# A weight unit of expert 28 loaded in sixteen transfers of eight partitions

## The chip, the cores and the metric

The kernel runs on one core of a Trainium2 chip. The metric is the device time of one execution in microseconds (us), the median of several executions.

## The reference

One decoder layer over 256 tokens of width 1024, in float32. A mixer (eight attention heads with forget gates beside a causal depthwise convolution) is added to the input; then comes a mixture of 32 experts, of which each token uses four:

```python
hn = rmsnorm(h, norm_ffn_g)
for e in range(32):                       # gates: softmax over the top 4 logits, else 0
    g, u = split(hn @ w_gu[e] + b_gu[e])  # w_gu[e]: 1024 x 2048
    act = (clip(u) + 1.0) * (min(g, 7) * sigmoid(1.702 * g))
    out += gates[:, e] * (act @ w_down[e] + b_down[e])   # w_down[e]: 1024 x 1024
return rmsnorm(h + out, norm_final_g)
```

An expert has 12 MB of weights, all 32 have 384 MB, and each is read once.

## The kernel before, in words

The mixer and the routing take the first 130 us or so. Then TensorE goes through the experts in order. For each it gathers up to 64 of its tokens, multiplies them with the expert's weights, and adds the results to the residual in PSUM. TensorE's stream is written out by hand in the functions `up`, `down`, `bias`, `gather_rows`, `scatter` and so on (L1484 to L1742); nearly all of its matmuls are recorded at one line, L1223, the helper `mm`.

The weights come in **units** of 1 MB: 128 partitions by 8 KB. An expert has eight units for its first matrix (`up`) and four for its second (`down`). `SEQUENCE` lists the units in order of use; the last two experts are interleaved: up of 30, up of 31, down of 30, down of 31. The units go into `ring`, 22 places of one unit each in SBUF. TensorE counts the units that it has finished with in the semaphore `units_used`; the sync engine (SP) waits for a place to be free and then issues the next load (loop at L466 and on, issue at L445).

A **load** is one DMA of one or more neighbouring units (`load_sizes`, L121): four units for most experts (packets of 32 KB to a partition), two from expert 28 on (`FINE_FROM` = 336, the first unit of expert 28; packets of 16 KB), one for the last ten units. A load that wraps around the end of the ring is cut in two (`pieces`). Twenty semaphores `load_full` serve the loads in turn; `landed(k)` is the count at which load k is all there, 16 for each DMA. TensorE waits for it in `arrived_unit` (L1564) before the first unit of the load. So a unit that landed can be used only once its whole load has landed.

All of these DMAs are issued on one queue, SP's. A DMA over 128 partitions is dealt to all sixteen DMA engines, eight partitions each, and each engine goes through its share of the queue by itself: none waits for another. A load has landed when the last engine is through with its share. The program's own instructions are fetched over the same engines (queues q8 and q14 of the profile).

After the last expert, both token blocks are normalised with `final_gain` (a last DMA on SP, L490) and written out (L504, L507).

Of the kernel before, what the change touches and what calls it, by code (L numbers as in the profile page):

```python
# [34 lines left out]
P = 128  # L35
# [16 lines left out]
def hybrid_layer(nc, x, norm_mix_g, w_in, b_f, b_glu, w_dw, b_dw, ln_g, ln_b, w_out, norm_ffn_g,  # L52
# [27 lines left out]
    UP_UNITS, DOWN_UNITS = KB, FB // 2  # L80
    UNITS = UP_UNITS + DOWN_UNITS
# [12 lines left out]
    SPARES = (UP_SPARE, DOWN_SPARE, ROW_SPARE)  # L94
# [3 lines left out]
    SINGLES, FINE_UP_TO, FINE_FROM = (UNITS * 2 + 8, UNITS * 3 + 2), UNITS * 8, UNITS * (E - 4)  # L98
# [14 lines left out]
    def unit_at(n):  # L113

        return FIRST_LAP.index(n) if n < LAP_END else (n - LAP_END) % RING

    def used_for(n):

        return FIRST_LAP[n - LAP_END] + 1 if n < LAP_END + RING else n - RING + 1
# [16 lines left out]
    LOADS = [(sum(SIZES[:k]), size) for k, size in enumerate(SIZES)]  # L136
    FIRSTS = {first: k for k, (first, _) in enumerate(LOADS)}
    LOAD_SEMS = 20

    def pieces(k):  # L140

        first, size = LOADS[k]
        size_here = min(size, RING - unit_at(first))
        return [(first, size_here)] + ([(first + size_here, size - size_here)] if size_here < size else [])

    def landed(k):

        return 16 * sum(len(pieces(j)) for j in range(k % LOAD_SEMS, k + 1, LOAD_SEMS) if LOADS[j][0] not in SPARES)

    assert all(sum(LOADS[k - LOAD_SEMS]) <= used_for(sum(LOADS[k]) - 1) for k in range(LOAD_SEMS, len(LOADS)))  # L150


# [2 lines left out]
    with ExitStack() as ctx:  # L155
# [3 lines left out]
        def sem(name):  # L159
            return ctx.enter_context(nc.semaphore(name))  # L160
# [127 lines left out]
        piece_in = {name: sem(f"{name}_in") for name in PIECES[2:]}  # L288
        load_full = [sem(f"load_full{s}") for s in range(LOAD_SEMS)]
        units_used, spare_in = sem("units_used"), sem("spare_in")  # L290
# [91 lines left out]
        def _(sp):  # L382
# [14 lines left out]
            for name in PIECES[2:]:  # L397
                if name.startswith("out"):
                    first = D_ATT if name == "out_conv" else 0
# [21 lines left out]
            def rows_of(first, size):  # L421

                e, u = SEQUENCE[first]
                return weight_rows(e, u, size)

            def weight_rows(e, u, size):
                if u < UP_UNITS:
                    g, b = u // 4, u % 4
                    return w_gu[e, 4 * P * g:4 * P * (g + 1), :].rearrange("(p b) n -> p b n", b=4)[:, b:b + size, :]
                f = 2 * (u - UP_UNITS)  # L430
                return w_down[e, :, :].rearrange("(p b) n -> p b n", b=FB)[:, f:f + 2 * size, :]

            def ring_rows(first, size, rows):
                return ring[:, unit_at(first) * UNIT:(unit_at(first) + size) * UNIT].rearrange("p (b n) -> p b n", b=rows)

            def load(k):

                for first, size in pieces(k):
                    from_ = rows_of(first, size)
                    if first == LAST_UNIT:  # L440
                        halves_ = ring_rows(first, size, from_.shape[1])
                        sp.dma_start(halves_[:, 0, :], from_[:, 0, :]).then_inc(load_full[k % LOAD_SEMS], 16)
                        sp.dma_start(halves_[:, 1, :], from_[:, 1, :]).then_inc(last_row_in, 16)
                        continue
                    sp.dma_start(ring_rows(first, size, from_.shape[1]), from_).then_inc(load_full[k % LOAD_SEMS], 16)  # L445

# [19 lines left out]
            for k, (first, size) in enumerate(LOADS):  # L466
                if first >= UNITS * E:
                    break
                if first in SPARES:
                    continue  # L470
                if first >= LAP_END:
                    sp.wait_ge(units_used, used_for(first + size - 1))
                elif first in released:
                    for used in released[first]:
                        sp.wait_ge(*used)
                load(k)
                if first == FIRST_LAP[2 * CONV_SLOT]:
                    sp.wait_ge(bgu_ready, 2)
                    load_spare_row(0)
                if first == FIRST_LAP[2 * KEYS_SLOT]:  # L480
                    load_up_spare()
                if first == FIRST_LAP[2 * PIECE_SLOT["out_conv"] + 1]:
                    load_down_spare_rest()
                if first == LAP_END - 1:
                    sp.wait_ge(route_done, 2)
                    load_spare_row(1)
                    load_down_spare()
# [4 lines left out]
            def extra(e, r, o):  # L492

                sp.wait_ge(units_used, o * UNITS + UNITS * E)
                for k, (first, size) in enumerate(LOADS):
                    if first >= UNITS * E:
                        from_ = weight_rows(e, first - UNITS * E, size)
                        sp.dma_start(ring_rows(first, size, from_.shape[1]), from_).then_inc(load_full[k % LOAD_SEMS], 16)

# [721 lines left out]
        def _(pe):  # L1221
# [342 lines left out]
            def arrived_unit(n, o=None):  # L1564

                if n in SPARES:
                    pe.wait_ge({UP_SPARE: up_spare_in, DOWN_SPARE: down_spare_in, ROW_SPARE: spare_in}[n], 32)
                elif n in FIRSTS:
                    k = FIRSTS[n]
                    pe.wait_ge(load_full[k % LOAD_SEMS], landed(k) if o is None else o * 16 + landed(k))  # L1570
# [213 lines left out]
```

## Time and profile before

| | us |
|---|---|
| median of 3 runs (lowest to highest) | 1038.83 (1038.70 to 1039.03) |
| profiled execution, its own time | 1038.4 |
| its span, first to last instruction | 1036.7 |
| TensorE busy | 1006.8 (97%) |
| share of the sixteen DMA engines in use | 96.7% by SP's queue |
| granted TensorE clock, mean | 0.994 of full speed |

The span is 1.7 us shorter than the time of its own execution, and that execution is 0.4 us under the median. Sums below are made against the span and carried over to the median. TensorE is busy nearly all the time, and so are the DMA engines. Which of the two holds the other up changes along the way, and that can be read only stretch by stretch.

### The profile page before, as it was taken

How to read it: one execution, taken by the hardware profiler on the slowest of the kernel's cores; microseconds unless marked ns; L12 is line 12 of the kernel's file. 1: busy time of each engine (PE TensorE's matmuls, PEld its weight loads, DVE VectorE, ACT ScalarE, POOL GpSimd, SP SyncE). 2: the span in 40 equal slices, each digit the busy share in tenths (PEclk: the TensorE clock that was granted, in tenths of full speed). 3: DMA queues.
4: the chain of work that ended last, by engine and by line, in shares of the span. 5: the costliest groups of instructions: out<-in, count | busy, mean ns of one | idle time of the engine just before them, and what ended most of it. 6: DMA issues, size and time to landing. Idle time of an engine off the chain costs nothing.

```text
span 1036.7 us, 11001 instructions
## 1 busy us (share of the span) xinstructions
PE 1006.8 (97%) x4821; PEld 398.2 (38%) x4822; DVE 242.2 (23%) x532; ACT 163.3 (16%) x303; POOL 15.0 (1%) x28
## 2 busy tenths in 40 slices
PE   9999999999999999999999999899999999899997
PEld 7875534333333333333333333333333333233332
DVE  3995341211011111111111212111111112011112
ACT  6144321111011111111110111010111101011102
POOL 4000000000000000000000000000000000000000
PEclk9999999999999999999999999999999999999999
DMA  9995789999999999999999999999999999999995
GB/s 309 391 421 198 277 342 399 417 415 428 427 426 434 426 434 428 435 425 434 426 435 426 435 427 431 432 429 428 433 429 429 433 428 431 425 428 426 425 422 223
DMA packets 34987, 421.62 MB, mean 407 GB/s; under 512 B 4237, under 2 KB 8633, under 8 KB 14714
## 3 DMA queue, kind: packets, MB, share of 16 engines
q1 hardware_dynamic: 33370, 420.57, 96.7%
q8 instruction: 39, 0.64, 0.2%
q10 hardware_dynamic: 1568, 0.33, 0.2%
q14 instruction: 10, 0.08, 0.0%
HBM read 419.82 MB, written 1.05 MB: 406 GB/s over the span
## 4 chain that ended last, share of the span: by engine, by line
PE 71%; DMA 21%; DVE 7%; ACT 1%; issue 0%; DVEq 0%; ACTq 0%
PE work L1223 60%; DMA ring<-in_w_gu 21%; PE resid L1223 7%; DVE main L917 4%; PE work L1531 1%; PE work L1605 1%; PE work L1561 0%; DMA main<-in_x 0%; PE work L1342 0%; PE work L1252 0%; PE work L1441 0%; DVE main L924 0%; DVE ring L896 0%; DVE ring L927 0%; DVE main L971 0%
## 5 line engine op out<-in xcount | busy, mean ns | idle before, releaser
L1223 PE MATMUL work<-ring,main 128*64 128x512 f32 (+1 forms) x3080 | 687.0, 596 | 17.4 <-DMA ring<-in_w_gu 15.9
L1223 PEld LDWEIGHTS work<-ring,main 128*64 128x64 f32 (+1 forms) x3080 | 219.1, 138 | 460.7 <-issue 411.3
L1126 DVE TENSOR_SCALAR main<-work 128x512 f32<-128x512 f32 x32 | 22.1, 692 | 554.5 <-PE work L1223 554.5
L757 ACT ACTIVATE main<-main 128x512 f32<-128x512 f32 x32 | 20.2, 632 | 434.6 <-DVE main L1126 434.6
L1223 PE MATMUL work<-ring 128*128 128x256 f32 (+2 forms) x308 | 71.8, 403 | 0.9 <-DVE ring L927 0.8
L1223 PE MATMUL resid<-main 128*128 128x512 f32 (+1 forms) x136 | 68.0, 618 | 0.8 <-ACT main L820 0.8
L1223 PE MATMUL work<-bgu_rows,ident 128*64 128x512 f32 (+1 forms) x260 | 61.0, 587 | 0.8 <-DVE main L1126 0.8
L1223 PEld LDWEIGHTS work<-ring 128*128 128x128 f32 (+1 forms) x308 | 55.6, 186 | 15.7 <-issue 8.7
L775 ACT ACTIVATE main<-work 64x512 f32<-64x512 f32 x60 | 35.5, 592 | 126.9 <-PE work L1223 126.2
L1119 DVE TENSOR_SCALAR lent<-count,place,gates 128x64 f32<-128x64 f32 x68 | 17.9, 310 | 155.3 <-PE work L1561 147.5
L917 DVE SCALAR_TENSOR_TENSOR main<-ring,main 128x256 f32<-128x256 f32 x116 | 46.6, 480 | 1.3 <-ACT main L631 1.1
L1223 PE MATMUL work<-main,select 128*64 128x512 bf16 x360 | 44.0, 379 | 0.0
L1133 DVE SCALAR_TENSOR_TENSOR main<-main 128x512 f32<-128x512 f32 x32 | 34.1, 1066 | 1.1
L1223 PEld LDWEIGHTS work<-main,select 128*64 128x64 bf16 x360 | 21.1, 110 | 29.7 <-issue 17.9
L762 ACT ACTIVATE main<-work 128x512 f32<-128x512 f32 x32 | 19.1, 597 | 72.3 <-PE work L1605 72.3
L1223 PEld LDWEIGHTS resid<-main 128*128 128x128 f32 (+1 forms) x136 | 19.6, 189 | 27.8 <-issue 27.8
L1223 PE MATMUL resid<-ring,main 128*128 128x512 f32 (+1 forms) x68 | 28.8, 571 | 0.0
L772 ACT ACTIVATE main<-work 128x256 f32<-128x256 f32 x17 | 6.5, 384 | 140.1 <-PE work L1561 140.1
L1223 PEld LDWEIGHTS work<-bgu_rows,ident 128*64 128x64 f32 x260 | 18.3, 137 | 24.4 <-issue 9.0
L1139 DVE TENSOR_TENSOR main<-work,cols 128x512 f32<-128x512 f32 x30 | 20.7, 691 | 13.1 <-PE work L1531 13.1
L1130 DVE TENSOR_TENSOR main<-main 128x512 f32<-128x512 f32 x32 | 22.2, 692 | 5.8 <-ACT main L757 5.8
L1531 PEld LDWEIGHTS work<-ident,lent 128*128 128x128 f32 x120 | 12.6, 140 | 24.3 <-issue 24.3
(200 smaller groups left out, 332.3 us busy)
## 6 DMA issues: line engine op xcount, KB each, us to landing
ring<-in_w_gu SPq DMA_DIRECT2D x33, 4096.0 KB, 39.3
ring<-in_w_gu SPq DMA_DIRECT2D x40, 2048.0 KB, 18.2
ring<-in_w_down SPq DMA_DIRECT2D x16, 4096.0 KB, 39.5
ring<-in_w_down SPq DMA_DIRECT2D x13, 2048.0 KB, 15.1
ring<-in_w_down SPq DMA_DIRECT2D x23, 1024.0 KB, 27.8
ring<-in_w_gu SPq DMA_DIRECT2D x22, 1024.0 KB, 18.9
ring<-in_w_gu SPq DMA_DIRECT2D x7, 3072.0 KB, 35.5
ring<-in_w_down SPq DMA_DIRECT2D x4, 3072.0 KB, 38.1
```

Of the source, the lines that this page charges most:

```text
L757: nc.scalar.activation(sig_h, gate_h, ACT.Sigmoid, scale=SWIGLU_ALPHA).then_inc(sig_ready, 1)
L762: nc.scalar.activation(to, work[:, act_bank(n), :], ACT.Copy).then_inc(act_t_ready, 1)
L775: return nc.scalar.activation(y_sb[buffer][h][parity * CAP:(parity + 1) * CAP, :], work[h * CAP:(h + 1) * CAP, bank, :], ACT.Copy)
L917: V.scalar_tensor_tensor(acc, u_pad[:, c, j:j + SEQ], dw_cols[:, c, j:j + 1], acc, ALU.mult, ALU.add)\
L1119: done = V.tensor_scalar(weighted[:, t, parity * CAP:(parity + 1) * CAP], count[:, bass.ds(r * CAP, CAP)], place[:, t, bass.ds(e, 1)], gat ...
L1126: V.tensor_scalar(gate_h, work[:, GATE_BANK, :], SWIGLU_LIMIT, None, ALU.min).then_inc(gate_clamped, 1)
L1130: V.tensor_tensor(sig_h, sig_h, gate_h, ALU.mult).then_inc(glu_ready, 1)
L1133: V.scalar_tensor_tensor(gate_h.rearrange("p (b j) -> p j b", b=4), up_h.rearrange("p (j b) -> p j b", b=4), 1.0, sig_h.rearrange("p (j b) ...
L1139: V.tensor_tensor(tok_t.rearrange("p (h b) c -> p b h c", b=4), work[:, OUT_BANK, :].rearrange("p (b h c) -> p b h c", b=4, h=2), cols[:, ...
L1223: return nc.tensor.matmul(out_, lhsT, rhs, start=start, stop=stop, skip_group_check=True)
L1531: last = nc.tensor.transpose(work[:, OUT_BANK, b * P:(b + 1) * P], tok_rows[:, b // 2, b % 2 * P:(b % 2 + 1) * P], ident[:, :])
L1605: last = nc.tensor.transpose(work[:, act_bank(n), j * P:(j + 1) * P], gate_h[:, j * P:(j + 1) * P], ident[:, :])
```

## The change

Load 336 (units 0 and 1 of expert 28, 2 MB) was one DMA of 128 partitions with 16 KB each. Now its first unit is one DMA of 128 partitions with 8 KB each, and its second unit is sixteen DMAs, each of eight partitions with 8 KB each. All seventeen count on the load's semaphore; `landed` counts them. Bytes, places and order stay as they were. A DMA over eight partitions is dealt to eight engines, one partition each.

```diff
+    BY_EIGHTS = (FIRSTS[FINE_FROM],)
+    EIGHT = 8
...
+    def transfers(k):
+
+        return len(pieces(k)) + (P // EIGHT if k in BY_EIGHTS else 0)
+
     def landed(k):
 
-        return 16 * sum(len(pieces(j)) for j in range(k % LOAD_SEMS, k + 1, LOAD_SEMS) if LOADS[j][0] not in SPARES)
+        return 16 * sum(transfers(j) for j in range(k % LOAD_SEMS, k + 1, LOAD_SEMS) if LOADS[j][0] not in SPARES)
...
                 for first, size in pieces(k):
                     from_ = rows_of(first, size)
+                    if k in BY_EIGHTS:
+                        to = ring_rows(first, size, size)
+                        sp.dma_start(to[:, 0:size - 1, :], from_[:, 0:size - 1, :]).then_inc(load_full[k % LOAD_SEMS], 16)
+                        for p in range(0, P, EIGHT):
+                            sp.dma_start(to[p:p + EIGHT, size - 1, :], from_[p:p + EIGHT, size - 1, :]).then_inc(load_full[k % LOAD_SEMS], 16)
+                        continue
```

## Rows read from the trace of the kernel before

**Rows 1.** The page: busy time of TensorE, DMA packets, and queues (packets, MB, share).
```profile
PE 1006.8 (97%) x4821; PEld 398.2 (38%) x4822; DVE 242.2 (23%) x532; ACT 163.3 (16%) x303; POOL 15.0 (1%) x28
...
q1 hardware_dynamic: 33370, 420.57, 96.7%
q8 instruction: 39, 0.64, 0.2%
```

**Rows 2.** The chain that ended last, 840 to 905 us: start, us, what.
```profile
849.29 3.61 PE work L1223 x16
852.90 0.02 issue
852.92 43.88 DMA ring<-in_w_gu
896.79 0.04 issue
896.84 8.35 PE work L1223 x29
```

**Rows 3.** The same chain, shares by line, 905 us to the end.
```profile
by line: PE work L1223 79.1%; PE resid L1223 9.4%; PE work L1531 1.8%; PE work L1605 1.8%; PE work L1561 1.0%; DVE main L1205 1.0%; ACT work L577 0.9%; DVE main L1212 0.6%; ACT main L831 0.5%; DVE main L1126 0.5%; ACT main L820 0.5%; issue 
```

**Rows 4.** Waits of the whole span, then of 905 us to the end: total us, times, longest.
```profile
PEld work L1223 <- DMA ring<-in_w_gu: 25.1, 12, 3.4
PE work L1223 <- DMA ring<-in_w_gu: 15.9, 11, 2.6
...
PEld work L1223 <- DMA ring<-in_w_gu: 0.8, 2, 0.5
```

**Rows 5.** Stretches: us, busy of PE, PEld, DVE, ACT, POOL, clock, DMA share, GB/s.
```profile
895.00:920.00 25.00, 23.16 (x104) 8.02 (x106) 4.59 (x9) 2.65 (x5) 0.00 (x0) 0.93 1.01 429
920.00:945.00 25.00, 25.00 (x122) 8.79 (x120) 4.52 (x10) 2.57 (x5) 0.00 (x0) 1.00 1.00 425
945.00:970.00 25.00, 25.00 (x122) 8.84 (x120) 3.74 (x5) 3.02 (x5) 0.00 (x0) 1.00 1.01 427
```

**Rows 6.** Issue L445 at 864.9 us (load 336), then at 941.5 us: issue ns, us to landing.
```profile
L445 SPq DMA_DIRECT2D ring<-in_w_gu x1: 328/328/328, 864.9 to 864.9; - x1
...
DMA to landing us min/median/max: 46.5/46.5/46.5
...
L445 SPq DMA_DIRECT2D ring<-in_w_gu x1: 2452/2452/2452, 941.5 to 941.5; - x1
...
DMA to landing us min/median/max: 43.9/43.9/43.9
```

**Rows 7.** TensorE in order of time: start, us, line, operation, tiles, count [idle before].
```profile
919.04 13.95 PE L1223 MATMUL work<-ring,main 128*64 128x512 f32 x64
...
982.17 7.09 PE L1223 MATMUL work<-ring,main 128*64 128x512 f32 x32
...
985.41 0.38 PEld L1223 LDWEIGHTS work<-ring,main 128*64 128x64 f32 x4 [0.47 <-DMA ring<-in_w_gu]
```

**Rows 8.** DMA share (tenths) and GB/s in 40 slices of 1016 to 1027 us.
```profile
DMA  9998999998777775566445454554444220000000
GB/s 372 417 447 358 432 462 432 372 402 328 328 313 313 313 298 238 238 253 238 179 179 194 179 209 179 209 209 194 179 179 164 119 104 30 30 0 0 0 0 0
```

**Rows 9.** Queues in 538 to 542 us, then in 59.3 to 60.0 us.
```profile
q8 instruction: 1, 0.02, 1.7%
...
q10 hardware_dynamic: 8, 0.01, 3.4%
```

**Rows 10.** SP: short DMAs of L391 (issue ns), order of time at 866 to 900 us, waits at 860 to 1010 us.
```profile
L391 SPq DMA_DIRECT2D ring<-in_w_dw x2: 316/366/417, 3.4 to 3.8; - x2
...
870.51 12.24 SPq L445 DMA_DIRECT2D ring<-in_w_gu  x3
887.07 4.14 SPq L445 DMA_DIRECT2D ring<-in_w_down  x2
894.31 0.33 SPq L445 DMA_DIRECT2D ring<-in_w_gu  x1
...
SPq L445 <- PE work L1223: 105.6, 26, 8.2
```

**Rows 11.** Issues by size: count, KB each, median us to landing.
```profile
result<-main SPq DMA_DIRECT2D x2, 256.0 KB, 2.0
ring<-in_w_gu SPq DMA_DIRECT2D x22, 1024.0 KB, 18.9
```

More of the change, by code:

```diff
@@ L144, in pieces @@
         return [(first, size_here)] + ([(first + size_here, size - size_here)] if size_here < size else [])
+    def transfers(k):
+        return len(pieces(k)) + (P // EIGHT if k in BY_EIGHTS else 0)
     def landed(k):
-        return 16 * sum(len(pieces(j)) for j in range(k % LOAD_SEMS, k + 1, LOAD_SEMS) if LOADS[j][0] not in SPARES)
+        return 16 * sum(transfers(j) for j in range(k % LOAD_SEMS, k + 1, LOAD_SEMS) if LOADS[j][0] not in SPARES)
+    assert all(len(pieces(k)) == 1 and LOADS[k][1] > 1 and LOADS[k][0] % UNITS < UP_UNITS for k in BY_EIGHTS)
     assert all(sum(LOADS[k - LOAD_SEMS]) <= used_for(sum(LOADS[k]) - 1) for k in range(LOAD_SEMS, len(LOADS)))
```

## The prediction, made before the result was known

> **What bounds the kernel now.** I read the page first. TensorE is busy 97% of the span and SP's DMA queue fills 96.7% of the sixteen engines [rows 1]; as averages these say only that both are nearly full. So I went to the chain that ended last. Until 896.8 us it comes back once in two experts to a weight load: its last such piece runs from 852.92 for 43.88 us and ends in TensorE's start at 896.84 [rows 2]. That stretch is bound by the DMA engines. From 905 us to the end the chain has no DMA in it at all: 79.1% is TensorE at the experts' matmuls, and the rest is TensorE's other work and the closing normalisation [rows 3]. The waits say the same. TensorE waited 15.9 us for loads in the whole span, 11 times; after 905 us it waited for none, and only two weight loads (which run ahead of the matmuls) waited, 0.8 us together [rows 4]. In the stretches 920 to 945 and 945 to 970 us TensorE is busy 25.00 of 25 us, at full clock, while the DMA engines are full too, at 425 to 427 GB/s [rows 5].
>
> The reason for the switch at 897 us is the size of the loads. The loads are smaller from expert 28 on, so a unit no longer waits for three neighbours. The DMA engines are no faster than before.
>
> The changed load is number 336. It was issued at 864.9 us and landed 46.5 us later, at 911.4 [rows 6]; TensorE first uses it at 919.04 [rows 7]. Everything that the change touches thus lies behind the last DMA wait of TensorE, in the part that TensorE bounds. What matters is how much room is left there. The tightest place I find is the fourth load of expert 30, issued at 941.5 and landed 43.9 us later, at 985.4 [rows 6]. Its first matmul is the 17th of the 32 that begin at 982.17 and take 7.09 us: 982.17 + 16 x 7.09 / 32 = 985.7. The weight load before it did wait 0.47 us, until 985.41, and no matmul was held up [rows 7]. So the room is 0.3 us there. At every other load behind the changed one it is more.
>
> **When a load lands.** It lands with its last engine, and the engines don't run together. At the end of the stream the share of busy engines falls from full to a half between 1018.7 and 1021.2 us, stays near a half until 1024.5, and reaches nothing at 1025.1 [rows 8] (slices of 0.275 us). So there is an early group of about eight engines and a late group of eight, some 4 us behind. A cause is in the trace: 39 instruction fetches of 16 KB on queue q8 [rows 1]. One of them takes 1.7% of 16 engines x 4 us = 1.1 us of one engine [rows 9]. Some 33 fetches fall after 150 us, when the stream hardly pauses any more; if only eight engines serve them, each loses 33 / 8 x 1.1 = 4.5 us. That is about the gap.
>
> **Which group gets the extra bytes** decides the sign. The kernel has two other transfers that are dealt to eight engines (8 KB each, issued on ScalarE's queue, q10). The first shows as 8 packets in 59.3 to 60.0 us [rows 9]. No view names a packet's engine. But on a busy engine the next packet starts where the last one ended, so the packet records can be strung into sixteen chains. I did that around this transfer: the engine that served the third q8 fetch is none of those that carry its packets, and neither are the two engines that were furthest behind at that time, as the first two fetches would leave them. I take it that the eight-row transfers use the group without fetches, the early one. The records before and after an idle queue can't be strung together, so this is a likely reading and no certain one.
>
> The Trainium skill ("DMA: Bandwidth & Descriptors", on why a DMA increments its semaphore by 16) says that such a transfer from SP uses the lowest-numbered engines, as many as divide its rows. The eight packets agree with the count of eight; which numbers they are, no row shows, and the page doesn't say which engines fetch instructions.
>
> **The change part by part.**
>
> *Bytes.* The second unit puts 128 KB on each of eight engines instead of 64 KB on each of sixteen. At 425 GB/s for sixteen engines [rows 5] one moves 26.6 KB/us (thousand bytes), so 65,536 bytes are 2.5 us. The early group gets 2.5 us later, the late group 2.5 us earlier. From load 336 on the late group (gap about 4 us) is then ahead of or level with the early one, and loads land 1.5 to 2 us sooner. Value in the span: 0, since no matmul waits there. What it adds is room at the 985 us place, 0.3 us before and about 2 us after.
>
> *Sixteen completions instead of one.* Below, nothing: completions of the neighbouring loads already pass between packets, and the share stays at 1.00 or more with 1 MB and 2 MB loads mixed [rows 5]. Above, each of the sixteen could hold its engines for the whole 2.0 us that a store on an idle queue takes from issue to landing [rows 11]; sixteen of them would be 32 us. I take nothing, as loads queued behind each other are the nearest row, and keep up to 0.1 us each (1.6 us) for the range.
>
> *SP's issue time.* Seventeen issues instead of one. The nearest short DMAs took SP 316 and 417 ns [rows 10], so 16 x 0.37 = 5.9 us more; SP is free of the load at about 871.2 instead of 865.3 us. Next in its queue is load 338, issued at 870.51 before: 0.7 us late. In 860 to 1010 us SP waited 105.6 us for TensorE to free places [rows 10], so it catches up at the next wait. Its lead over the landing is 46.5 us [rows 6]. Cost 0. If the cover of that lead were gone, it would be the 5.9 us.
>
> *Room in the queue.* Later issues of SP take up to 2.45 us [rows 6] where others take 0.33, so the queue has a limit. The early engines get 16 x 2 more entries (a packet and a completion each) in place of 8. SP will be held up sooner, in 870 to 905 us, and stand some loads further back. With more than 40 us queued before it I expect that half of that remains. Cost 0; the bound above is in the rivals.
>
> *TensorE's wait* is for one higher count, the same instruction. Cost 0.
>
> Sum: 0 on a span of 1036.7, thus 1038.4 for the profiled execution, 1038.8 for the median. In other executions the room of 0.3 us may be used up (they took up to 0.4 us longer), and the change could then give back up to 0.4 us. I stay with 1038.8.
>
> **The rivals.**
>
> *Slower: the late group gets the bytes.* If the low eight are the late ones, or some of them are, every load from 336 on lands 2.5 us later. It decides where the room is under 2.5 us, above all at 985.4: the matmul due at 985.7 starts at 987.9, and 2.5 - 0.3 = 2.2 us go straight through to the end; later loads then have the 2.2 us more. 1038.8 + 2.2 = 1041.0. For it: my chains are strung by nearness in time. Against it: three fetches of three, all on engines outside the eight. 10%.
>
> *Slower: small transfers or a full queue.* Each of the sixteen holds its engines for some time of its own, or SP, held up by the queue's limit, lets the engines run dry. At the bound of 2.0 us each it is 32 - 0.3 = 31.7 us, 1070.5; it shows from 0.15 us each on (16 x 0.15 = 2.4). Against it: the landings of 22 loads of 1 MB, 18.9 us after issue in the median [rows 11], with full engines, which shows many in flight at once. 5%. The Trainium skill (same page, the rules for kernel authors) says that transfers under 64 KB pay mostly overhead and that its measured 64 KB transfer took 0.95 us; each of the sixteen is just 64 KB. By that, run one after the other, they would take 15.2 us. The trace speaks against its use here, since it is a figure for one transfer alone.
>
> *Faster: earlier landings count.* If the median execution, unlike the profiled one, waits in the last 140 us, the 1.5 to 2 us come off: 1037.0. Against it: the three runs lie within 0.33 us, and the profiled one is 0.4 us under them. 4%; more than 0.2% only if other loads gain too, 2%.
>
> *It doesn't do what it says.* The eight-row DMAs are spread over sixteen engines, and nothing moves: 1038.8. The eight packets of q10 are against it. 4%.
>
> **How the numbers follow.** My forecast has 77%, the other cases 10, 5, 4 and 4. 0.2% is 2.1 us, about what a measurement of this kernel can tell from no change. Within it lie the forecast, the last two rivals but for 2%, and a part of the first (2.2 us is just over it; 2% of its 10). Faster 0.02, same 0.85, slower 0.13. The forecast's own range is 1038.2 to 1039.3. With the bound of 1.6 us for the completions, the earlier landings, and the first rival it is 1037.4 to 1041.1.
>
> **What would show it.** In the profile after: the last DMA wait of TensorE still at 896.8; no wait of 905 us or later; load 336 landing at about 909.5; the load issued near 941.5 landing near 983.7 and no 0.47 us before its weight load; in the last stretch the groups' two falls in share closer together, the last at about 1023.5. A DMA wait of about 2 us near 986 us, with landings 2.5 us later, would prove my reading of the groups wrong. SP issues of some us each between 871 and 905 are expected and should cost nothing.

## The result and the profile after

Over four executions the changed kernel took 1047.01 us in the median (1045.92 to 1047.87), the kernel before 1038.93 us (1038.70 to 1039.47) in the same job. The ratio is 1.0073 with a 95% interval of 1.0056 to 1.0089: 8.1 us slower, where no change was forecast. The profiled execution took 1047.87 us with a span of 1046.0, 9.3 us more than the span of before. The lines of code have moved: L445 is now L458, L1223 is L1236, the changed load is issued on L449 (its first unit) and L451 (the sixteen transfers).

The page, its busy times and queues, against [rows 1]:
```profile
PE 1007.4 (96%) x4821; PEld 397.2 (38%) x4822; DVE 242.3 (23%) x532; ACT 163.0 (16%) x303; POOL 14.9 (1%) x28
...
q1 hardware_dynamic: 33626, 420.57, 96.6%
```
TensorE does the same work in 0.6 us more (1006.8 us before). SP's queue moves the same bytes in 256 more packets and is as full as before. So all but 0.6 of the 9.3 us is idle time of TensorE, and yet no engine of the DMA has become idle. The page alone shows no cause.

The chain that ended last, 840 us to the end (start, us, what), against [rows 2] and [rows 3]:
```profile
854.92 41.85 DMA ring<-in_w_gu
...
918.75 1.08 SPq L458
919.83 0.04 issue
919.88 45.17 DMA ring<-in_w_gu
...
998.17 4.12 SPq L458
1002.29 0.36 issue
1002.65 30.29 DMA ring<-in_w_down
```
Up to 896.8 us it is the chain of before: the load on it was issued 2.0 us later (854.92 against 852.92), but TensorE starts within 0.02 us of the same time (896.82 against 896.84). Then it has DMA in it twice more, where it had none after 905.

TensorE's matmuls after 905 us that waited for a load (start, us, line, operation, tiles, count [idle before and its releaser]):
```profile
921.31 3.65 PE L1236 MATMUL work<-ring,main 128*64 128x512 f32 x16 [2.21 <-DMA ring<-in_w_gu]
925.85 3.65 PE L1236 MATMUL work<-ring,main 128*64 128x512 f32 x16 [0.89 <-DMA ring<-in_w_gu]
930.74 3.65 PE L1236 MATMUL work<-ring,main 128*64 128x512 f32 x16 [1.24 <-DMA ring<-in_w_gu]
935.64 3.65 PE L1236 MATMUL work<-ring,main 128*64 128x512 f32 x16 [1.25 <-DMA ring<-in_w_gu]
960.12 3.65 PE L1236 MATMUL work<-ring,main 128*64 128x512 f32 x16 [0.83 <-DMA ring<-in_w_gu]
965.09 3.65 PE L1236 MATMUL work<-ring,main 128*64 128x512 f32 x16 [1.32 <-DMA ring<-in_w_gu]
1032.98 3.65 PE L1236 MATMUL work<-ring,main 128*64 128x512 f32 x16 [0.30 <-DMA ring<-in_w_down]
```
Seven waits, 8.0 us; before there was none [rows 4]. The first is for the changed load itself, which lands at 921.3 instead of 911.4 us. The next load lands at 925.8 (issued 883.2, 42.6 us to landing); before it was 916.3 (870.5 + 45.8). It is 9.5 us late too. From there on the loads come only as fast as the engines move them, and TensorE meets the delay in pieces.

Where the delay arises, the table of stretches shows (columns as in [rows 5]; the last two are the DMA engines' share and GB/s). The first line is of the kernel before, the others are of the kernel after:
```profile
900.00:920.00 20.00, 20.00 (x98) 7.00 (x96) 4.59 (x9) 2.65 (x5) 0.00 (x0) 0.98 1.00 425
...
860.00:900.00 40.00, 37.17 (x168) 12.35 (x168) 5.32 (x13) 4.50 (x8) 0.00 (x0) 0.96 1.00 427
900.00:920.00 20.00, 19.09 (x92) 6.61 (x88) 4.60 (x9) 2.67 (x5) 0.00 (x0) 0.99 1.01 272
920.00:945.00 25.00, 20.32 (x98) 7.19 (x100) 4.51 (x9) 2.54 (x5) 0.00 (x0) 1.00 1.00 425
945.00:970.00 25.00, 22.85 (x110) 7.47 (x108) 1.21 (x2) 1.67 (x3) 0.00 (x0) 1.00 1.01 425
```
Between 900 and 920 us the engines are as busy as ever (share 1.01) and move 272 GB/s, not 425. This is the stretch in which the sixteen transfers are served. The packet records say how: a packet of 8 KB takes 314 ns in the median from 895 to 900 us and 656 ns from 908 to 912; in those four microseconds one of 16 KB takes 613 ns in the kernel before and 1288 ns here. Those of 16 KB belong to whole loads. Of the 323 packets of 8 KB or more that began between 904 and 920 us, every one took over 15% longer than packets of its size take at the full rate (313, 614 and 915 ns for 8, 16 and 24 KB); of those that began from 896 to 903 us none did. So packets on all sixteen engines slow down, not only those of the changed load.

The working for the whole: (425 - 272) x 20 / 425 = 7.2 us lost by the rate, minus the room of 0.3 us, is 6.9 of the 9.3 us measured in the span. That leaves 2.4 us. The 2.5 us for the bytes on engines that carry more, if a late one is among them, would fill them, but that this is their source is not shown (see "Which group gets the bytes" below). The question for the experiments was what halves the rate.

SP's queue in order of time (start, us, line, operation, count), against [rows 10]:
```profile
866.95 0.33 SPq L449 DMA_DIRECT2D ring<-in_w_gu  x1
867.32 15.86 SPq L451 DMA_DIRECT2D ring<-in_w_gu  x16
883.23 11.78 SPq L458 DMA_DIRECT2D ring<-in_w_gu  x3
```
The sixteen issues take 15.9 us, the last two 2.4 us each. SP is held up, as expected. But the first slow packet begins at 903.0 us, some 20 us after the last of these issues, and no engine runs dry, so this is not the cause.

### The profile page after: what moved, and what is told of

Same layout as the page of the kernel before. It is cut to its first block, busy times and chain, and to the rows that moved or that the text cites. A ratio compares the mean times of both kernels' runs of the same rounds, so it can differ in the third digit from the quotient of the medians.

```text
span 1046.0 us, 11017 instructions
## 1 busy us (share of the span) xinstructions
PE 1007.4 (96%) x4821; PEld 397.2 (38%) x4822; DVE 242.3 (23%) x532; ACT 163.0 (16%) x303; POOL 14.9 (1%) x28
## 3 DMA queue, kind: packets, MB, share of 16 engines
HBM read 419.82 MB, written 1.05 MB: 402 GB/s over the span
## 4 chain that ended last, share of the span: by engine, by line
PE 69%; DMA 28%; DVE 1%; SPq 0%; ACT 0%; issue 0%; DVEq 0%; ACTq 0%
PE work L1236 59%; DMA ring<-in_w_gu 25%; PE resid L1236 7%; DMA ring<-in_w_down 3%; PE work L1544 1%; PE work L1618 1%; SPq L458 0%; DMA main<-in_x 0%; PE work L1574 0%; PE work L1355 0%; PE work L1265 0%; PE work L1454 0%; DVE main L984 0%; DVE main L964 0%; DVE main L1218 0%
## 5 line engine op out<-in xcount | busy, mean ns | idle before, releaser
L1236 PE MATMUL work<-ring,main 128*64 128x512 f32 (+1 forms) x3080 | 686.6, 595 | 26.1 <-DMA ring<-in_w_gu 24.3
L1236 PEld LDWEIGHTS work<-ring,main 128*64 128x64 f32 (+1 forms) x3080 | 217.9, 138 | 471.0 <-issue 408.8
L1236 PE MATMUL work<-ring 128*128 128x256 f32 (+2 forms) x308 | 71.8, 403 | 0.9 <-issue 0.8
L1236 PE MATMUL resid<-main 128*128 128x512 f32 (+1 forms) x136 | 68.9, 624 | 0.8 <-ACT main L833 0.8
L1236 PE MATMUL work<-bgu_rows,ident 128*64 128x512 f32 (+1 forms) x260 | 61.0, 587 | 0.8 <-DVE main L1139 0.8
L1236 PEld LDWEIGHTS work<-ring 128*128 128x128 f32 (+1 forms) x308 | 55.6, 186 | 15.7 <-issue 8.7
L1236 PE MATMUL work<-main,select 128*64 128x512 bf16 x360 | 44.0, 379 | 0.0
L1236 PEld LDWEIGHTS work<-main,select 128*64 128x64 bf16 x360 | 21.2, 110 | 29.7 <-issue 17.9
L1236 PEld LDWEIGHTS resid<-main 128*128 128x128 f32 (+1 forms) x136 | 19.9, 191 | 27.8 <-issue 27.8
L1236 PE MATMUL resid<-ring,main 128*128 128x512 f32 (+1 forms) x68 | 28.8, 571 | 0.0
L1236 PEld LDWEIGHTS work<-bgu_rows,ident 128*64 128x64 f32 x260 | 18.3, 137 | 24.4 <-issue 9.0
```

What stands on the lines that cost most here:

```text
L1236: return nc.tensor.matmul(out_, lhsT, rhs, start=start, stop=stop, skip_group_check=True)
```

## The experiments

All of them change only how load 336 is brought in (2 MB, two units of 128 partitions). Three groups of four were run, with the kernel before at 1038.84, 1038.83 and 1038.88 us. In all twelve profiles the DMA engines stay full from 900 to 945 us (share 0.94 to 1.05 in every stretch read). The tables below have the columns of [rows 5].

**First group: is it the layout on one side, or the number of transfers?** In the kernel after, each small transfer writes eight neighbouring partitions from eight neighbouring rows. First, both sides four apart, so that eight transfers stay in partitions 0 to 63 and eight in 64 to 127:
```diff
-                            sp.dma_start(to[p:p + EIGHT, size - 1, :], from_[p:p + EIGHT, size - 1, :]).then_inc(load_full[k % LOAD_SEMS], 16)
+                            base = 32 * (p // 32) + p % 32 // EIGHT
+                            sp.dma_start(to[base:base + 29:4, size - 1, :], from_[base:base + 29:4, size - 1, :]).then_inc(load_full[k % LOAD_SEMS], 16)
```


> The sixteen transfers take eight partitions each that are four apart (base, base + 4, ... base + 28) on both sides, instead of eight neighbours; same bytes, same count, same eight engines per transfer. Theory A (eight engines write into neighbouring partitions of SBUF at once and get into each other's way there): the slow packets go, time within 1 us of before, 1038.5 to 1039.5. Theory B (eight engines read neighbouring rows of 8 KB in HBM at once): the same, so this run alone doesn't part A from B. Theory C (each small transfer costs its engines time, wherever it writes): as the changed kernel, about 1047. Theory D (the late engines got the extra bytes): 1041 to 1047, with landings 2.5 us later than before.

Measured: 1046.16 us (1045.47 to 1047.61), ratio 1.0076 [1.0059, 1.0093]. In the time it is the kernel after. In the table of stretches it is not:
```profile
900.00:903.00 3.00, 3.00 (x18) 0.95 (x14) 0.00 (x0) 0.00 (x0) 0.00 (x0) 1.00 1.05 442
904.00:911.00 7.00, 7.00 (x38) 2.69 (x34) 2.81 (x4) 1.63 (x3) 0.00 (x0) 1.00 1.05 234
914.00:918.00 4.00, 2.52 (x12) 0.63 (x8) 0.86 (x4) 1.41 (x3) 0.00 (x0) 1.00 0.99 233
```
The first transfers, to partitions 0 to 63, run at the full rate (8 KB packets at 312 ns, 88 of them from 900 to 904 us). From about 904 us, with the first transfer to partitions 64 to 127, it is 234 GB/s. From 914 to 918 us only the engines that lag furthest are still at the small transfers (10 packets of 8 KB begin in it), and the rate is as low as before.

Then only one side four apart:
```diff
+                            sp.dma_start(to[base:base + 29:4, size - 1, :], from_[p:p + EIGHT, size - 1, :]).then_inc(load_full[k % LOAD_SEMS], 16)
```


> Only the side in SBUF takes partitions four apart; the side in HBM reads eight neighbouring rows as in the changed kernel (so the rows of this unit stand in other partitions than they should; bytes and times are the same). Theory A (writes into neighbouring partitions): fast, 1038.5 to 1039.5. Theory B (reads of neighbouring rows): slow, about 1047. Theory C (small transfers as such): slow, about 1047.

```diff
+                            sp.dma_start(to[p:p + EIGHT, size - 1, :], from_[base:base + 29:4, size - 1, :]).then_inc(load_full[k % LOAD_SEMS], 16)
```


> Only the side in HBM reads rows four apart; the side in SBUF writes eight neighbouring partitions as in the changed kernel (so the rows of this unit stand in other partitions than they should). Theory A (writes into neighbouring partitions): slow, about 1047. Theory B (reads of neighbouring rows): fast, 1038.5 to 1039.5. Theory C: slow, about 1047.

And the load in two DMAs of 128 partitions:
```diff
-                        for p in range(0, P, EIGHT):
-                            sp.dma_start(to[p:p + EIGHT, size - 1, :], from_[p:p + EIGHT, size - 1, :]).then_inc(load_full[k % LOAD_SEMS], 16)
+                        sp.dma_start(to[:, size - 1, :], from_[:, size - 1, :]).then_inc(load_full[k % LOAD_SEMS], 16)
```


> The load is cut in two as in the change, but its second unit is one DMA over 128 partitions: no transfer of eight partitions is left. All theories expect the time of before, 1038.5 to 1039.5; another time would put the cause on the cut itself (8 KB instead of 16 KB packets, one more completion).

Measured: 1045.95 us, ratio 1.0070 [1.0054, 1.0087], with the SBUF side alone four apart; 1046.29, 1.0077 [1.0060, 1.0094], with the HBM side alone; and 1039.42, 1.0006 [0.9996, 1.0016], with two whole DMAs, which keep 422 GB/s from 900 to 920 us. The first shows the two halves of the run above (399 GB/s at 900 to 903, 258 at 904 to 911); the second is slow throughout (289 GB/s at 900 to 920). The stretch in the second and in the run with two whole DMAs:
```profile
900.00:920.00 20.00, 18.17 (x89) 6.65 (x87) 4.61 (x9) 3.39 (x6) 0.00 (x0) 1.00 1.01 289
...
900.00:920.00 20.00, 20.00 (x98) 7.08 (x96) 4.59 (x9) 3.39 (x6) 0.00 (x0) 1.00 1.00 422
```
What follows: the HBM side changes nothing, neither kind of neighbour alone is the cause, and splitting the load costs nothing if each part spans 128 partitions. Which partitions are written matters, and so far in step with the half of SBUF.

**Second group: which partitions, and does it need small transfers?** One half of the partitions comes in one DMA of 64 rows, the other in sixteen transfers of eight rows:
```diff
-                        sp.dma_start(to[:, 0:size - 1, :], from_[:, 0:size - 1, :]).then_inc(load_full[k % LOAD_SEMS], 16)
-                        for p in range(0, P, EIGHT):
-                            sp.dma_start(to[p:p + EIGHT, size - 1, :], from_[p:p + EIGHT, size - 1, :]).then_inc(load_full[k % LOAD_SEMS], 16)
+                        sp.dma_start(to[64:P, :, :], from_[64:P, :, :]).then_inc(load_full[k % LOAD_SEMS], 16)
+                        for n in range(P // EIGHT):
+                            base = 0 + 32 * (n % 8 // 4) + n % 4
+                            sp.dma_start(to[base:base + 29:4, n // 8, :], from_[base:base + 29:4, n // 8, :]).then_inc(load_full[k % LOAD_SEMS], 16)
```


> Sixteen transfers of eight partitions again, 1 MB in all, but all of them to partitions 0 to 63 (both units of the load, rows four apart); partitions 64 to 127 of both units come in one DMA of 64 rows by 16 KB, ahead of them. Theory E: each partition of SBUF is written through one of sixteen ways, the way that is one engine's alone in a DMA of 128 partitions; the eight engines of the small transfers own the ways of partitions 0 to 63, so packets of the small transfers stay at 309 to 320 ns; the 64-row DMA has two writers per way, eight ways, four packets of about 1220 ns in place of 613. The eight engines carry 2.5 us more bytes and the 64-row DMA costs 2.4 us: landings up to 5 us later, 5 - 0.3 = 4.7 at most, time 1041 to 1043.5. Theory C (small transfers as such, wherever they write): packets near 620 ns again, time 1046 or above.

The mirror of it, with `to[0:64]` in one DMA and `base = 64 + ...`:

> The mirror image: the sixteen transfers write partitions 64 to 127 (rows four apart, both units), and partitions 0 to 63 come in the one DMA of 64 rows. Same count, bytes, sizes and engines. Theory E: the small transfers now go through the other eight engines' ways: 16 packets of about 620 ns on their engines (9.9 us) and half speed for the other eight meanwhile; landings about 9.9 us later, time 1047 to 1049, 4 to 6 us above the run with partitions 0 to 63. Theory C: no difference between the two runs.

As the first, but the sixteen write neighbours (`base = EIGHT * (n % 8)`, `base:base + EIGHT`):

> As the run with partitions 0 to 63, but each small transfer takes eight neighbouring partitions instead of rows four apart. Theory E: eight engines then meet on the two ways of eight neighbours, though all ways are their own group's: packets well above 320 ns, while the eight engines that don't take part keep 613 ns for 16 KB; slower than the run with rows four apart by 2 to 10 us. Theory C: no difference.

And no small transfer at all:
```diff
+                        for rows in (slice(64, P), slice(0, 64)):
+                            sp.dma_start(to[rows, :, :], from_[rows, :, :]).then_inc(load_full[k % LOAD_SEMS], 16)
```


> No small transfer at all: the load is two DMAs of 64 partitions by 16 KB each, upper half first. Each uses all sixteen engines. Theory E: all sixteen write through eight ways, two writers to each: four packets of about 1220 ns per DMA, 9.8 us for the load in place of 4.9, less where engines are in different halves at a time; no engine has more bytes than before. Landings up to 4.9 us later, time up to 1043.4, and at least 1040. Theory C: 1039, as nothing is small.

Measured: 1048.32 us (ratio 1.0090 [1.0073, 1.0107]), 1054.39 (1.0150 [1.0118, 1.0181]), 1050.20 (1.0111 [1.0094, 1.0128]) and 1050.64 (1.0110 [1.0093, 1.0127]). All four are slower than the kernel after. The last, with two DMAs of 1 MB and nothing small, costs 11.8 us, more than the sixteen small transfers of the kernel after (8.1). It also misses what theory E allowed it (at most 1043.4), as the first does (at most 1043.5): more than the load's own packets must be slowed. The stretches of the last:
```profile
890.00:898.00 8.00, 5.45 (x28) 1.98 (x26) 0.00 (x0) 0.00 (x0) 0.00 (x0) 1.00 1.03 437
899.00:924.00 25.00, 19.04 (x83) 6.71 (x80) 3.74 (x5) 1.82 (x3) 0.00 (x0) 0.86 1.01 212
926.00:945.00 19.00, 14.76 (x68) 4.64 (x66) 0.86 (x4) 1.56 (x3) 0.00 (x0) 1.00 1.00 425
```
From 899 to 924 us it is 212 GB/s, half of 425, and packets take twice their time (16 KB: 1240 ns in the median). At that rate the load's own 2 MB would take 9.9 us; the slow stretch lasts 25 us, in which 5.3 MB are moved, so some 3 MB of other loads are slow with it. Of the first:
```profile
900.00:917.00 17.00, 12.76 (x62) 5.08 (x60) 3.75 (x5) 1.82 (x3) 0.00 (x0) 0.92 1.01 221
918.00:923.00 5.00, 5.00 (x22) 1.47 (x20) 0.00 (x0) 0.00 (x0) 0.00 (x0) 1.00 1.00 426
```
It is 221 GB/s as long as the 64-row DMA is in work, and 426 from 918 us, although small transfers to partitions 0 to 63 are still being served then (9 packets of 8 KB after 920 us, 313 ns each). In the mirror the second part stays slow (292 GB/s at 917 to 930), in the one with neighbours too (340). So size and number of the transfers, the completions and SP's issues are not the cause; the slow rate is there with two large DMAs and absent with small ones four apart in 0 to 63.

What is left is a reading, inferred and not seen, since no view names a packet's engine. In it each engine has partitions that it writes at the full rate, those that it writes in a whole DMA of 128 partitions; an engine that writes to others makes all of them slow. In a DMA of 64 rows, sixteen engines take four rows each, so that they can't all be at their own.

The Trainium skill ("DMA: Bandwidth & Descriptors", on the descriptor swizzle) says that in a DMA of 128 partitions engines 0 to 7 write partitions 0 to 63, each engine four neighbours and the four 32 further up, and engines 8 to 15 the others. By that and by its count of engines, and if the rows go to the engines in order, eight rows four apart in 0 to 63 put each of engines 0 to 7 on its own partitions. Eight neighbours belong to two engines, so that at most two of the eight can be on their own, and of rows in 64 to 127 none is. The runs order themselves that way (420, 285 and 211 GB/s in the third group).

**Third group: the small transfers without the rest.** In the first three of these kernels the other half of load 336 is left out, 1 MB less. Each of the eight engines used carries for this load what it carried before (128 KB), so no engine is later by bytes. The other eight have 128 KB less, 4.9 us of their time, which could hide a cost in the time of the kernel but not in the rate.
```diff
+                        for n in range(P // EIGHT):
+                            base = 0 + 32 * (n % 8 // 4) + n % 4
+                            sp.dma_start(to[base:base + 29:4, n // 8, :], from_[base:base + 29:4, n // 8, :]).then_inc(load_full[k % LOAD_SEMS], 16)
```


> Leaves out partitions 64 to 127 of both units of load 336 (1 MB isn't loaded). Partitions 0 to 63 of both units come in sixteen transfers of eight partitions four apart; there is no 64-row DMA. Each of the eight engines carries 128 KB, as before; the other eight nothing for this load. Theory E (sixteen ways into SBUF, one engine's own each; a packet on another's way halves the two) and theory F (the same ways, but while any engine writes to a partition that isn't its own, the packets of all sixteen take twice as long): packets at 309 to 320 ns, 425 GB/s throughout, time 1038 to 1039.5. Theory C (small transfers as such): slow packets, 1042 or more.

With neighbours in 0 to 63:

> The same bytes and the same partitions as the run before it in this group (partitions 64 to 127 of load 336 left out), but each of the sixteen transfers takes eight neighbouring partitions. Theory F: half rate from the first small packet of the earliest engine to the last of the latest, 16 x 0.62 + about 7 us of spread = 17 us, so about 8 us lost on each engine; with 5 us fewer bytes on the eight engines that take no part and as many on the others, landings 5 to 8 us later, time 1043 to 1047. Theory E: slow packets on the eight engines alone, 613 ns for 16 KB on the others. Theory C: no difference from rows four apart.

Four apart, but in 64 to 127:

> The mirror image: partitions 0 to 63 of load 336 are left out, and partitions 64 to 127 come in sixteen transfers of eight partitions four apart, carried by the same eight engines. Same count, sizes and bytes. Theory E: both groups of eight slow, as each small packet meets the owner of its way. Theory F: half rate for all, about 17 us as with neighbours, time 1043 to 1047. Theory C: no difference from partitions 0 to 63.

The last kernel is the first of these with one more transfer behind the sixteen, to eight neighbours in the other half:
```diff
+                        sp.dma_start(to[64:64 + EIGHT, 0, :], from_[64:64 + EIGHT, 0, :]).then_inc(load_full[k % LOAD_SEMS], 16)
```


> As the run with partitions 0 to 63 four apart, and one transfer more, of partitions 64 to 71 of the first unit, behind the sixteen (the rest of 64 to 127 is left out). Theory F: while that one packet of 8 KB per engine is under way on any of the eight engines, everything runs at half rate: up to 8 x 0.62 = 5 us in several short pieces, up to 2.5 us lost; time 1038.5 to 1041, and packets of 16 KB well above 613 ns on many engines. Theory E: two ways alone are touched, a loss of at most 0.3 us, and most packets of 16 KB stay at 613 ns.

Measured, with a line of each table of stretches. Four apart in 0 to 63: 1038.64 us (1037.03 to 1040.00 in ten executions), ratio 0.9997 [0.9987, 1.0006].
```profile
900.00:916.00 16.00, 16.00 (x76) 5.69 (x74) 3.74 (x5) 1.83 (x3) 0.00 (x0) 0.93 1.00 420
```
Neighbours in 0 to 63: 1045.56 us, 1.0073 [1.0056, 1.0089].
```profile
899.00:916.00 17.00, 16.37 (x78) 6.07 (x76) 3.74 (x5) 1.82 (x3) 0.00 (x0) 0.95 1.02 285
```
Four apart in 64 to 127: 1049.03 us, 1.0102 [1.0086, 1.0119].
```profile
900.00:917.00 17.00, 10.81 (x58) 4.31 (x56) 3.73 (x5) 1.82 (x3) 0.00 (x0) 0.89 0.99 211
```
In this run the first long wait is for a load that stands ahead of the changed one in the queue, 3 MB of expert 27's `down`:
```profile
916.57 5.31 PE L1236 MATMUL work<-ring,main 128*64 128x512 f32 x16 [6.19 <-DMA ring<-in_w_down]
```
It landed 52.8 us after its issue; before it was 44.7 us, and TensorE did not wait for it. So the small transfers also slow what was queued before them: the engines are some microseconds apart in the queue, and the first are at the small transfers while the last still work on that load.

The same sixteen transfers, with the same bytes and the same completions, cost nothing, 6.7 us or 10.2 us, by the partitions alone. And the partitions 0 to 63 themselves are not at fault: with neighbours, or with the 64-row DMA of the second group, they are slow too. What remains is the pairing of engine and partition. Its milder form, theory E, in which only the engines that meet are slowed, is ruled out by the run with neighbours: all 272 packets of 8 KB or more that began in it from 902 to 916 us took over 15% longer than at the full rate. Those of 16 KB, which belong to whole loads, took 724 ns or more, where theory E had 613 ns for the eight engines that take no part.

The loss again follows roughly from the rate. With neighbours (425 - 285) x 17 / 425 = 5.6 us, less the room of 0.3, is 5.3 against 5.0 in its span (1041.7 - 1036.7; its profiled execution was the fastest of the four). In 64 to 127 it is 8.3 against 7.8 (1044.5 - 1036.7). With the two halves of the second group it is (425 - 212) x 25 / 425 - 0.3 = 12.2 against 15.3 (1052.0 - 1036.7); that profiled execution was the slowest of its four, and the rest is not explained.

One transfer astray behind the sixteen:
```profile
900.00:907.00 7.00, 6.84 (x32) 2.33 (x34) 0.00 (x0) 0.00 (x0) 0.00 (x0) 1.00 0.98 414
907.00:909.00 2.00, 2.00 (x18) 1.01 (x16) 1.54 (x3) 0.96 (x2) 0.00 (x0) 1.00 1.00 340
909.00:917.00 8.00, 8.00 (x36) 2.82 (x34) 2.19 (x3) 0.86 (x2) 0.00 (x0) 1.00 1.01 416
```
Measured: 1038.62 us (1037.75 to 1041.72 in ten executions), 1.0000 [0.9990, 1.0009]. The rate falls to 340 GB/s for two microseconds. Of the 54 packets of 8 KB or more that begin in them 22 take over 15% longer (16 KB up to 1155 ns, 8 KB up to 528 ns), more than the eight packets of the one transfer. The 0.4 us lost, (425 - 340) x 2 / 425, is no more than the time can show. (The profiled execution took 1041.72 us, but it was late by some 3 us before any of this: SP issued the first of the sixteen at 870.22 us, against 866.83 in the run without the last transfer.) This speaks for a slowdown that all engines share and against one confined to the engines or partitions touched, but it is the weakest of the runs: its effect is in the records and not in the time.

## Why the prediction was wrong

**What held.** The reading of the bound held: TensorE reaches 896.8 us as before, and all that was lost was lost by loads that landed after it. SP was held up sooner and ran later than forecast (15.9 us of issues for 5.9 taken), at no cost: the kernel with the sixteen transfers four apart in 0 to 63 spends 10.7 us on its issues and loses nothing. The engines never ran dry. TensorE's wait for a higher count cost nothing. And the room behind 905 us is small: what the loads lose comes through nearly whole (6.9 us by the rate and 9.3 in the span, 5.3 and 5.0, 8.3 and 7.8). The 0.3 us itself lies below what these sums can confirm.

**The step that failed** is "Sixteen completions instead of one", taken as 0, since loads queued behind each other were the nearest row. As a price of completions the 0 was right: sixteen transfers to partitions 0 to 63, four apart, cost nothing (0.9997 [0.9987, 1.0006]). What had no term in the sum is the place to which they write. All loads that I compared with span 128 partitions; none of the rows could show what a DMA to fewer partitions does to the rate of the others. The step let a small transfer cost its own engines at most, and left the rate of all other loads at 425 GB/s; it was 272 for 20 us. In this kernel it is 7.2 us for sixteen transfers, 0.45 us each. That lies between the bounds of 0 and 2.0 us each, and above the 0.1 us that I kept for the range. I had narrowed the range by arguing one possible cause of a cost away, and the cost had another cause.

**The rival that came nearest** is the one of small transfers, from 0.15 us each on, in its size and sign. Its mechanism, engines held by each small transfer or left dry by a slow SP, is not what happens. The chance of 5% was too small for a kind of transfer of which the trace had two instances, of 8 KB each.

**Which group gets the bytes** was read partly wrong. With the packet records strung into sixteen chains, the times at which each engine finished the last loads show two of the sixteen some 10 us or more behind the first in the kernel after; before, the whole spread was 7.3 us. That would fit eight engines of which two belong to the late ones, and then the first rival's 2.5 us would stand in the sum beside the 7.2. Two runs speak against all of it: those with one side alone four apart put the same bytes on eight engines, and at 289 GB/s from 900 to 920 us the rate alone makes (425 - 289) x 20 / 425 - 0.3 = 6.1 us, where their spans grew by 7.3 (SBUF side) and 6.7 (HBM side). That leaves 1.2 and 0.6 us, not 2.5. No run isolates this share, so the source of the 2.4 us in the kernel after stays open. The forecast of a gain in landings (load 336 at 909.5 us) did not come: it landed at 921.3.

**The wide range** of 1037.4 to 1041.1 does not follow from its terms, which give 1037.0 with earlier landings and 1041.0 with the first rival. For the result this makes no difference: it lies 6 us above either upper end.

**The warning that was set aside.** The Trainium skill ("DMA: Bandwidth & Descriptors", the rules for kernel authors, with the page's 0.95 us for 64 KB) gave an estimate of 15.2 us if they ran one after the other. Its sign is right, and its size is no further off than my 0, but the run with the same sixteen transfers at no cost shows that the overhead of a small transfer is not what was paid here. The Trainium skill's page "SBUF — State Buffer", on the DMA port swizzle, says that a DMA's bandwidth depends on how many of sixteen ports its partitions reach, and that partitions 32 apart share a port, which I left out as it speaks of one transfer's own speed. Here the trace goes further than that: the transfers slow the packets of whole loads on the other engines (16 KB from 613 to 1288 ns), those queued before them too.

**What stays open** is the mechanism: why engines writing to partitions that are not theirs, if that is it, slow all sixteen, whether one that writes there alone would do it or only one that meets the owner, and why neighbours cost a third of the rate (285 GB/s) where the other half costs a half (211 GB/s). The Trainium skill ("DMA: Bandwidth & Descriptors", on back-pressure in remote DMA) describes a saturated SBUF port that clogs the path back to every engine that shares it. It says so of transfers between cores; these are not, and no run here can see the path. No faster kernel was found or tried: in the last 140 us TensorE and the DMA engines are both full, and every run that moved bytes between engines was slower or the same.

## What to carry to other kernels

Load SBUF tiles with DMAs that span all 128 partitions; two DMAs of 64 partitions each cost this kernel 11.8 us for 2 MB, sixteen of eight cost 8.1, two of 128 cost nothing that can be told. If a DMA of eight partitions must be used, four apart within 0 to 63 was the form that cost nothing here; other sizes, and stores, were not tried. Then look at the GB/s of the stretch, since the share of busy DMA engines stays at 1.00 while the rate halves. And where the trace has no instance of a new kind of transfer, keep its bound in the range: cost it by what it may do to all others in flight, not only by its own bytes and completions.

## What the runs showed that I had not expected

- Two 64-partition DMAs bring the rate of all sixteen engines from 437 to 212 GB/s for 25 us, with the engines 101% busy; 24 KB packets of other loads go from 914 to 1868 ns in the median.
- Sixteen transfers of 64 KB each, queued behind each other, are free when they are written four partitions apart in partitions 0 to 63 (420 GB/s in the stretch), and halve the rate of everything (211 GB/s) in 64 to 127.
- The slow rate begins and ends within a microsecond or two of the transfers that bring it: 442 to 234 GB/s between 903 and 904 us in the kernel with both sides four apart, 340 GB/s for only 2 us with one transfer astray.
- A load that stands ahead of the small transfers in the queue is slowed as well: 52.8 us from issue to landing in place of 44.7.
- Which rows of HBM a small transfer reads made no difference (1046.16, 1045.95 and 1046.29 us).
